# Measured durations for the planner of a two-block transformer kernel

## What is computed

```
# block 1
h = rmsnorm(x); z = h @ w_in
a  = softmax attention, 8 query heads and 2 key heads of 128, RoPE, normed q and k
b  = 12 heads of 64 in three dilations, banded softmax with relative bias, merged by logsumexp
x += (sigmoid(ga) * (a @ w_out_a) + sigmoid(gb) * (b @ w_out_b)) @ w_out
x += relu(rmsnorm(x) @ w_ff1)^2 @ w_ff2                      # hidden 4096
x += sigmoid(rmsnorm(x) @ w_ple_gate) * (p @ w_ple);  x = rmsnorm(x)
# block 2
x += 0.5 * swiglu(rmsnorm(x))                                # hidden 2816
x += [retention, 4 heads | differential attention, 4 heads of 2 x 64] @ w_out
x += attention to 256 memory rows, 4 heads of 256
x += 0.5 * swiglu(rmsnorm(x));  y = rmsnorm(x)
```

## Time and profile before

| | |
|---|---|
| Median of 3 runs | 2078.06 us (2077.78 to 2078.34) |
| Profiled execution | 2076.73 us, its span 2074.9 us |
| Mean granted TensorE clock | 0.994 of full speed |
| Busy: DVE | 1120.6 us (54%) |
| Busy: ACT | 892.3 us (43%) |
| Busy: POOL | 331.6 us (16%) |
| Matmuls | 9996 |
| Chain that ended last | PE 94%, DVE 4%, ACT 1% |

### The profile page before, as it was taken

How to read it: one execution, slowest core, us unless ns; L and a number is a source line. 1 busy time by engine, 2 the same in 40 slices (tenths; PEclk the granted TensorE clock), 3 DMA queues, 4 the chain that set the end, 5 groups by cost and what they waited for, 6 DMA issues and landing times.

```text
span 2074.9 us, 25532 instructions
## 1 busy us (share of the span) xinstructions
PE 2051.3 (99%) x9996; PEld 1720.1 (83%) x9996; DVE 1120.6 (54%) x1989; ACT 892.3 (43%) x1755; POOL 331.6 (16%) x319
## 2 busy tenths in 40 slices
PE   8999999999999999999999999999999999999997
PEld 6988888888888888878888888788898888888886
DVE  6446786444544344565443435787775664443434
ACT  5245564345433232553322225676664543232324
POOL 3003422032000000342110101231311021110102
PEclk9899999999999999999999999999999999999999
DMA  5112111243323232233323323223242032323222
GB/s 195 49 63 72 51 41 54 89 128 126 102 92 102 93 101 92 78 113 96 100 92 101 99 80 117 77 73 104 84 153 90 28 117 91 96 97 102 92 91 72
DMA packets 61637, 191.56 MB, mean 92 GB/s; under 512 B 6792, under 2 KB 14472, under 8 KB 61516
## 3 DMA queue, kind: packets, MB, share of 16 engines
q1 hardware_dynamic: 61516, 189.93, 28.7%
HBM read 187.69 MB, written 2.21 MB: 92 GB/s over the span
## 4 chain that ended last, share of the span: by engine, by line
PE 94%; DVE 4%; ACT 1%; issue 0%; DMA 0%; SPq 0%; DVEq 0%; ACTq 0%
PE bank L292 92%; PE bank L297 1%; DVE tmp L181 0%; DVE wl L469 0%; DVE work L190 0%; ACT rsq L178 0%; ACT wh L467 0%; DMA raw<-d_wts 0%; DVE tmp L184 0%; DVE x_sb L181 0%; DVE work L181 0%; DVE pd L184 0%; DVE rsq L184 0%; DVE pd L196 0%; ACT tmp L178 0%
## 5 line engine op out<-in xcount | busy, mean ns | idle before, releaser
L467 ACT ACTIVATE wh<-raw 128x512 fp32r<-128x512 f32 (+1 forms) x700 | 403.8, 610 | 921.2 <-PE bank L292 911.1
L292 PE MATMUL bank<-h_h,wh 128*128 128x512 f32 x1488 | 590.3, 397 | 7.2 <-ACT wh L467 6.2
L292 PE MATMUL bank<-h_l,wh 128*128 128x512 f32 x1488 | 581.7, 391 | 1.2 <-DVE h_l L184 1.2
L292 PE MATMUL bank<-h_h,wl 128*128 128x512 f32 x1488 | 581.1, 391 | 0.0
L469 DVE TENSOR_TENSOR wl<-raw,wh 128x512 fp32r<-128x512 f32 (+1 forms) x642 | 430.0, 695 | 61.5 <-ACT wh L467 39.5
L292 PEld LDWEIGHTS bank<-h_h,wh 128*128 128x128 f32 x1488 | 280.5, 188 | 68.6 <-ACT wh L467 6.2
L292 PEld LDWEIGHTS bank<-h_l,wh 128*128 128x128 f32 x1488 | 280.3, 188 | 61.1 <-DVE h_l L184 3.7
L292 PEld LDWEIGHTS bank<-h_h,wl 128*128 128x128 f32 x1488 | 280.2, 188 | 59.3 <-DVE wl L469 0.3
L469 POOL TENSOR_TENSOR wl<-raw,wh 128x256 fp32r<-128x256 f32 x114 | 95.1, 863 | 330.1 <-ACT wh L467 330.1
L202 POOL TENSOR_TENSOR tmp<-tmp,rstd 128x512 f32<-128x512 f32 x44 | 63.4, 1442 | 469.4 <-ACT tmp L178 469.4
L181 DVE TENSOR_TENSOR tmp<-bank,rstd 128x512 f32<-128x512 f32 x92 | 64.7, 706 | 118.1 <-PE bank L292 117.4
(11 more groups left out here) (473 smaller groups left out, 3499.4 us busy)
## 6 DMA issues: line engine op xcount, KB each, us to landing
raw<-d_wts SPq DMA_DIRECT2D x314, 512.0 KB, 3.5
raw<-d_wts SPq DMA_DIRECT2D x24, 384.0 KB, 3.0
x_sb<-d_xT SPq DMA_DIRECT2D x16, 256.0 KB, 5.4
raw<-d_wts SPq DMA_DIRECT2D x24, 128.0 KB, 2.0
d_yT<-x_sb SPq DMA_DIRECT2D x4, 384.0 KB, 2.9
tab<-d_ali SPq DMA_DIRECT2D x4, 256.0 KB, 4.1
tab<-d_dec SPq DMA_DIRECT2D x4, 256.0 KB, 3.8
mraw<-d_memT SPq DMA_DIRECT2D x8, 128.0 KB, 2.5
```

The lines of the kernel that those rows point to most:

```text
L292: bank.done = pe.add(lambda e: e.matmul(out, lhsT, rhs, start=first, stop=True, skip_group_check=True), n, w, waits)
L467: p.th = [Op(act, lambda e, c=c: e.activation(H[:, c], raw[:, c], FN.Copy), [p.load]) for c in (slice(o, min(o + 512, width)) for o in ran ...
```

## The change

The cost formulas get new constants. This concerns every helper that adds an instruction to ACT, DVE, POOL or PE, the two choices between DVE and POOL, the conversions of a panel in `parts_here()`, and the rule `behind` in `take()`. For PE the load of the stationary operand gets a cost of its own (0.111 us for 128 columns, else 0.06); it is added for stationary operands of 64 rows and 128 columns, and is a lower bound for others. One line of another kind: `handover()` sets only the first five tiles of `gz` free, not the eight of `more_z`. The diff:

```diff
--- before.py
+++ after.py
@@ -172,40 +172,40 @@
         return op
 
     def a_act(out, in_, func, *waits, **kw):
-        cost = 0.1 + 0.00082 * size(in_) + 0.06 * ("bias" in kw) + 0.08 * ("accum_out" in kw)
+        cost = 0.19 + 0.00085 * size(in_) + 0.06 * ("bias" in kw) + 0.19 * ("accum_out" in kw)
         if "scale" in kw and not isinstance(kw["scale"], float):
             cost += 0.1
         return act.add(lambda e: e.activation(out, in_, func, **kw), cost, waits)
 
     def v_tt(out, a, b, op, *waits):
-        return dve.add(lambda e: e.tensor_tensor(out, a, b, op), 0.065 + 0.00105 * size(a), waits)
+        return dve.add(lambda e: e.tensor_tensor(out, a, b, op), 0.14 + 0.00108 * size(a), waits)
 
     def v_stt(out, a, s, b, op0, op1, *waits, rev=False):
-        return dve.add(lambda e: e.scalar_tensor_tensor(out, a, s, b, op0, op1, reverse0=rev), 0.1 + 0.00105 * size(a), waits)
+        return dve.add(lambda e: e.scalar_tensor_tensor(out, a, s, b, op0, op1, reverse0=rev), 0.16 + 0.00108 * size(a), waits)
 
     def v_ts(out, a, s1, s2, op0, op1, *waits):
-        return dve.add(lambda e: e.tensor_scalar(out, a, s1, s2, op0, op1), 0.12 + 0.0006 * size(a), waits)
+        return dve.add(lambda e: e.tensor_scalar(out, a, s1, s2, op0, op1), 0.22 + 0.00053 * size(a), waits)
 
     def v_red(out, a, op, *waits, negate=False):
-        return dve.add(lambda e: e.tensor_reduce(out, a, X, op, negate=negate), 0.065 + 0.00105 * size(a), waits)
+        return dve.add(lambda e: e.tensor_reduce(out, a, X, op, negate=negate), 0.14 + 0.00108 * size(a), waits)
 
     def v_cp(out, a, *waits):
-        return dve.add(lambda e: e.tensor_copy(out, a), 0.065 + 0.00105 * size(a), waits)
+        return dve.add(lambda e: e.tensor_copy(out, a), 0.14 + 0.00108 * size(a), waits)
 
     def v_ttr(out, a, b, scale, first, op0, op1, acc, *waits):
-        return dve.add(lambda e: e.tensor_tensor_reduce(out, a, b, scale, first, op0, op1, acc), 0.08 + 0.00105 * size(a), waits)
+        return dve.add(lambda e: e.tensor_tensor_reduce(out, a, b, scale, first, op0, op1, acc), 0.22 + 0.00108 * size(a), waits)
 
     def v_rcp(out, a, *waits):
-        return dve.add(lambda e: e.reciprocal(out, a), 0.07 + 0.0063 * size(a), waits)
+        return dve.add(lambda e: e.reciprocal(out, a), 0.15 + 0.0063 * size(a), waits)
 
     def p_tt(out, a, b, op, *waits):
-        return pool.add(lambda e: e.tensor_tensor(out, a, b, op), 0.1 + 0.0022 * size(a), waits)
+        return pool.add(lambda e: e.tensor_tensor(out, a, b, op), 0.15 + 0.00235 * size(a), waits)
 
     def v_mul(out, a, s, *waits):
         return v_ts(out, a, s, None, ALU.mult, ALU.bypass, *waits)
 
     def p_mul(out, a, s, *waits):
-        return pool.add(lambda e: e.tensor_scalar(out, a, s, 1.0, ALU.mult, ALU.mult), 0.07 + 0.0012 * size(a), waits)
+        return pool.add(lambda e: e.tensor_scalar(out, a, s, 1.0, ALU.mult, ALU.mult), 0.17 + 0.0016 * size(a), waits)
 
     def sooner(waits, dve_cost, pool_cost):
 
@@ -214,11 +214,11 @@
 
     def e_tt(out, a, b, op, *waits):
         n = size(a)
-        return (v_tt if sooner(waits, 0.065 + 0.00105 * n, 0.2 + 0.0022 * n) else p_tt)(out, a, b, op, *waits)
+        return (v_tt if sooner(waits, 0.14 + 0.00108 * n, 0.25 + 0.00235 * n) else p_tt)(out, a, b, op, *waits)
 
     def e_mul(out, a, s, *waits):
         n = size(a)
-        return (v_mul if sooner(waits, 0.12 + 0.0006 * n, 0.17 + 0.0012 * n) else p_mul)(out, a, s, *waits)
+        return (v_mul if sooner(waits, 0.22 + 0.00053 * n, 0.27 + 0.0016 * n) else p_mul)(out, a, s, *waits)
 
     table = [None]
 
@@ -287,8 +287,13 @@
 
     def b_mm(bank, out, lhsT, rhs, *waits):
         first, w = opened(bank)
-        n = 0.0025 + size(rhs) / 2400
-        n = max(n, 0.055) if lhsT.dtype == F32R else max(4 * n, 0.108)
+        load, n = 0.111 if size(lhsT) == 128 else 0.06, size(rhs) / 2400
+        if lhsT.dtype != F32R:
+            n = max(4 * n + 0.01, 0.112)
+        elif lhsT.shape[0] == 64 and size(lhsT) == 128:
+            n += load
+        else:
+            n = max(n + 0.013, load)
         bank.done = pe.add(lambda e: e.matmul(out, lhsT, rhs, start=first, stop=True, skip_group_check=True), n, w, waits)
         return bank.done
 
@@ -446,8 +451,8 @@
     def parts_here(after):
 
         low = (dve if not first_parts else pool) if len(panels) < 3 else panels[-1].low
-        act.t = max(act.t, after) + 1.04
-        low.t = max(low.t, act.t - 0.5) + (2.4 if low is pool else 1.2)
+        act.t = max(act.t, after) + 1.26
+        low.t = max(low.t, act.t - 0.6) + (3.0 if low is pool else 1.39)
 
     def take(s):
 
@@ -460,7 +465,7 @@
         src = d["wts"][p.off:p.off + 128 * width].rearrange("(p n) -> p n", p=128)
         raw, p.H, p.L = raw_t[i % 3], wh_t[i % 3], wl_t[i % 3]
         H, L = p.H, p.L
-        behind = max(dve.t, pe.t) + 1.2 > max(pool.t, pe.t) + 2.4
+        behind = max(dve.t, pe.t) + 1.39 > max(pool.t, pe.t) + 3.0
         p.low = low = pool if (behind if i > 3 else i > 0) else dve
         p.cut = 256 if low is pool else 512
         p.load = Op(sp, lambda e: e.dma_start(raw[:, 0:width], src), [panels[i - 3].tl] if i >= 3 else [], raw_sem[i % 3])
@@ -1174,7 +1179,7 @@
         for t in list(pta) + qs[2:4] + pa.slots[4:8]:
             t.free = list(done_b["scores", 1])
         yield lambda: ("values", 1) in done_b
-        for t in list(outa) + gz.slots:
+        for t in list(outa) + gz.slots[0:5]:
             t.free = list(done_b["values", 1])
 
     def proj_rope(n0, gname, dst, finish):
```

## The result

| | before | after |
|---|---|---|
| Median | 2077.92 us (2076.35 to 2078.34) | 2107.6 us (2105.23 to 2108.47) |
| Ratio | | 1.0144, 95% interval [1.0132, 1.0156] |
| Profiled execution, its span | 2076.73 us, 2074.9 us | 2108.47 us, 2106.7 us |
| Mean granted TensorE clock | 0.994 | 0.988 |

The changed kernel is 1.4% slower, 29.7 us, where 2.6 us of gain were forecast; it lies outside the range and beyond rival C. The lines of helpers moved down by five: L292 is now L297, L467 is L472, L469 is L474.

A forecast was written before the change was run, and what follows sets the result against it. PE, busy 99% of the span, was taken to bound the kernel. Gains of 4.1 us against 1.5 us of new stalls gave net -2.6 us, a median of 2075.4 us; range 2069.0 to 2083.0 us.

The forecast's parts named there:

- rival C: Second block: DVE takes over POOL's panels and score chains queue behind conversions; +5.5 us, 2083.6 us; chance 0.14.
- point 2: PE's lower clock near 39 us, behind the first scores' gaps: half of 1.5 us regained, -0.75 us.
- Point 1: First scores, 36.36 to 37.55 us: PE's wait for DVE's low parts of two tiles goes, -0.95 us.
- Point 3: First block's attention: PE's wait for pa, behind an exponential booked too short, goes, -0.6 us.
- Point 4: Gate after the first MLP, 912 us: waits for h_h and h_l behind ACT's queue, half of 1.35 us, -0.7 us.
- Points 5 and 6: Second block's str0l wait, mem_hl meeting POOL, half of 1.2 us: -0.6; waits for mraw and pd: -0.5 us.
- Against it: Whole order placed anew: new misses where the plan is still wrong, two stalls of 0.75 us, +1.5 us.
- one stall of the listed size: 64-row scores matmuls, overbooked by up to 1.1 us: jobs taken for ready too early, priced as one stall.
- DVE gets more work: POOL-or-DVE choice for panels: wider margins give DVE some of POOL's 28 panels, mostly where PE has no wait.
- signs that I had listed as "wrong": PE waits in MLPs, changed clock over 60:100 us, waits' sum above 15 us, DVE busier by over 15 us.
- the first four reads of h: Part of PE's listed 13.1 us of waits: 1.2 us, counted outside what a better order could reach.
- D: POOL relieved, so two-input DVE operations run free of it; str0l's stall alone goes, 1.2 us, 2076.9 us; chance 0.06.

The follow-up runs named there:

- e10: The kernel before with weight panel 6's load issued a panel earlier on SP, and the change's `gz` line; 2079.3 us, ratio 1.0011.
- e3: The changed kernel without the 0.111 us surcharge for stationary operands of 64 rows; 2116.4 us, ratio 1.0184.
- e6: The changed kernel, with both banks of a differential head taken together before its two maps' matmuls are queued; 2100.8 us, ratio 1.0108.
- e11: The changed kernel with panel 6's load early, both banks taken together, and panel conversions from panel 134 on given to DVE; 2092.1 us, ratio 1.0072.

## Why the prediction was wrong

**What held.** The long pieces of 227 ns gained and lost nothing. DVE's busy time moved by 5 us, most durations stayed, and nothing was lost to the `gz` line, by the queues of e10. The clock did cost at the first scores, as point 2 had it.

**Point 1, the first scores, -0.95.** The sign failed, and this is the step that failed first: "SP's loads keep their places at panel steps, so no DMA moves against PE by more than a step". True of SP and PE, and beside the matter. What moved was ACT's order against a DMA that stood still: 11.00 us of idle ACT in front of qb000h. The row for it was there before: the 6.33 us of idle ACT at 42.17 us, behind qb010h. I had read the two small gaps of DVE's low parts and not asked what ACT was waiting for right behind them. The term was +7.9 us until the first scores, +10.7 by the end of the stretch, clock included.

**Point 2, the clock, -0.75, bounds of 1.5.** The lower level isn't tied to the place near 39 us. It came behind the new gaps at 925, 1501 and 1527 us, and at other places with no gap at all (0.84 over 60:100 in the trace of before, which I left out of the sum), some 13 us more of it in all. The step that failed is that I priced it for one place in the trace of before, instead of giving each new miss a share of it and the rest a range.

**Point 3, pa, -0.6.** The wait is 1.1 us after, 0.6 before.

**Point 4, the gate, -0.7, or as much again lost.** Lost, and more: PE waits 2.1 us for h_h, where the earlier trace rows had 1.0; +2.6 us with the clock behind it. The mechanism, queue order inside DVE, was the right one, the size was not.

**Points 5 and 6, str0l, mraw, pd, -1.1.** The waits for str0l and pd are gone; str1l's of 2.0 us stands in their place, and mraw's grew to 0.8. The mechanism of point 5 was named rightly, mem_hl beside POOL, but I gave it only the one stall that stood there. It returned as 3.1 us of waits for mem_hl itself.

**"Against it", +1.5, bounds 0 and 6.** This term carried the result. I took two misses of 0.75 us from the size of the stalls that a good order happened to have. The runs give its price: three nudges of the old planner cost 6, 15 and 24 us, four to sixteen times the 1.5. Every other order that was run was slower than this one, which had 13.1 us of waits in 2075. The stalls that are left in such an order are no measure of those that it avoids.

**64 rows, "one stall of the listed size".** The surcharge didn't cost this (e3). The split pairs did cost 4.3 us. e6 mends them by taking both banks first, so the plan's step between the two banks is where other matmuls came in. The old showed them side by side, and I took that for a property of the code, not of the order.

**"DVE gets more work".** False: 28 panels on POOL became 39. The wider margin was most likely outweighed by DVE's longer bookings, the very sentence that stood against rival C; no run took the two apart.

**Rivals.** C had the side and not the cause. DVE was not loaded more, POOL was; e11, where DVE does get the panels, is 5.8 us slower with waits for vml and mem_hl, which fits C's mechanism, but a redrawn order alone costs as much. That C's price was 5.5 is chance; its own eight stalls of 0.75 us make 6.0. Of the signs that I had listed as "wrong", two came: the waits' sum over 15 us (28.6), and another clock pattern (0.89 over 60:100, 0.84 before). A reading was off as well, without weight in the sum: "the first four reads of h" are three (0.9 us); the fourth of h_l's waits is the 0.35 us of point 4. D's rule shows in the rows of the second block's entry, wl at 1.44 us beside POOL's sums, 0.69 alone, and in mem_hl's median of 0.853 us against 0.474. D expected fewer such meetings; there were more. The Trainium skill (SBUF — State Buffer, Who interferes with whom) says that a DVE operation with two inputs in SBUF and a POOL operation that reads SBUF contend for a shared read interface. These rows agree as far as they go: either engine took longer in them (POOL's sums 1.74 us, 1.44 before).

## What to carry to other kernels

When a planner's numbers change, don't price the stalls that the present order still has; price a new order, by nudging the planner in two or three ways that mean nothing and seeing how far the time goes. Do the same for the noise: run kernels with equal queues, and see how far a stretch moves by itself. Look in the trace for idle time that ends in a DMA and costs nothing only because of what stands ahead of it on that engine: a plan that doesn't know of the transfer can put anything behind it. And where two operations are fast only side by side, make the code issue them together, so that no order can split them.

## What the hardware showed

- Behind gaps of PE of 0.6 to 2.1 us the granted clock fell to the lower level for several us (0.55 to 0.62 over three stretches of 4 to 7 us), in places where the kernel before held 1.00. It also fell where PE had no gap: to 0.57 over 179 to 187 us (after), right behind 64-row matmuls, and to 0.84 over 60 to 100 us (before). There it wasn't alike in two executions of the same queues (0.79 and 0.57 over 175 to 183 us). In the sum of the whole kernel the lower level cost nearly as much as the new waits: some 13 us beside 15.5.
- Two matmuls of 64 rows on the two halves start every 135 ns for 512 columns. Apart from each other three of them take 0.34, 0.23 us and the rest (1354.90, 1355.24, 1355.47 us, next at 1355.79), 0.89 us for three where six took 0.81.
- A DVE piece of 512 columns that takes 0.69 us took 1.44 beside POOL's sums of 512, whose own duration went from 1.44 us (the mean of 45 in the trace of before) to 6.94 / 4 = 1.74. A DVE scalar_tensor_tensor of 256 columns that takes 0.47 us took up to 1.48 beside POOL's row operations.
